# Up pass of a sparse expert layer: low parts made ahead of row fetches, row coefficients spread a group ahead

## Chip, cores and metric

The kernel runs on one core of one Trainium2 chip. The metric is the device time of one execution in microseconds. The median of three runs of the kernel before is 4072.21 us (4071.66 to 4079.16).

## What is computed

The reference is one block of a hybrid network for 1024 tokens of width 1024: an RG-LRU and an SSD mixer, then a feed-forward layer that picks experts. Only that last layer matters here:

```
def peer_ffn(h, w_q, sub_keys, expert_down, expert_up):
    ...
    idx = i1 * PEER_KEYS + i2          # 8 heads x 16 picks of 16384 experts, for each token
    g = jax.nn.softmax(cv, axis=-1)
    u = expert_down[idx]
    act = jax.nn.gelu(jnp.einsum('thkd,td->thk', u, xb).astype(jnp.float32), approximate=False)
    v = expert_up[idx]
    return jnp.einsum('thk,thkd->td', (g * act).astype(xb.dtype), v)
```

The expert tables have 16384 rows of 1024 float32. The last sum, over v, is the up pass, `experts_up`, the last stage of the kernel.

## The kernel before

The up pass treats the eight blocks of 128 tokens in three ways.

**Five dense blocks (640 tokens).** For them the sum over picks is a matrix product with the whole table. The table comes in 128 blocks of 128 experts. A block n = 4g + j belongs to group g of `GROUPS` = 32, with `GT` = 4 blocks each. SP loads the block (`up_raw`, two buffers) and its coefficients (`gelu_in` and `weights_in`, two buffers each; L2305, L2308, L2309). A load of `up_raw` waits until the low part of the block two before is made, a load of coefficients until the low part of the coefficients two before is made. For full precision each operand is split into a high and a low part:

- ScalarE makes `up_hi` (L2400) and `coef_hi` (L2402). Its copies for group g wait until TensorE is through with group g - 2.
- GpSimd makes `up_lo`, in `cut(g, j)` (L2352).
- VectorE multiplies the coefficients (L2466) and makes `coef_lo` (L2468), in `coefs(g, j)`.

TensorE works a group as ten slots (five blocks of tokens by two halves of the width). A slot is twelve matmuls (L2576; in group 0, L2557, the slots go in two halves of five, with the blocks of experts outside). A group begins when all four cuts and all four low parts of the coefficients are made. VectorE adds the slots of group g - 1 to `y_acc` in `add` (L2478; L2475 for group 0) while it prepares group g: slots 0 and 1 after block 0, slots 2 to 4 after block 1, slots 5 and 6 after block 2, slots 7 to 9 after block 3.

**Two blocks of tokens by rows on TensorE.** For each pick of each of 256 tokens one row of the table is gathered, the 128 rows of one token per fetch: `fetch(r)` (L2335) is an indirect DMA of 128 rows of 1024 float32 into one of `RING` = 6 tiles. TensorE takes four such tiles in `quad(n)` (L2538), rows 4n to 4n + 3, with 16 matmuls. Quad 2g stands after slot 0 of group g, quad 2g + 1 after slot 5. The coefficients of a quad are spread by VectorE in `spread_rows(n)` (L2445), into one of four buffers. A row fetch waits until the quad that read its tile before is done. After the 32nd quad ScalarE copies the sums away (`keep_rows`, L2390).

**One block of tokens on VectorE.** `fetch_own(c)` (L2345) gathers row c of 128 tokens into one of two tiles. `add_own(c)` (L2458; L2454 for the first) adds it on VectorE. An own fetch c waits until own add c - 2 is done. VectorE does own add 4(g - 1) + j right after `coefs(g, j)`.

All engines work their queues in order. The order on GpSimd is written out by hand (L2355 to L2382), and the change touches it. In group g of the loop GpSimd issues row fetches 8g - 2 to 8g + 1 (the first four) and 8g + 2 to 8g + 5 (the second four), and own fetches 4g - 2 to 4g + 1.

Of the kernel before, what the change touches and what calls it, by code (L numbers as in the profile page):

```python
# [2238 lines left out]
GT = 4  # L2239
# [3 lines left out]
def experts_up(m, inp, keep, scratch, out):  # L2243
# [6 lines left out]
    GROUPS = E1 // GT  # L2250
    SLOTS = 2 * ND
    BANKS = SLOTS // 2
    NP = NA - 1
# [5 lines left out]
    with ExitStack() as st:  # L2259
# [38 lines left out]
        with nc.Block() as block:  # L2298
            @block.sync
            def _(sp):  # L2300
                for n in range(E1):
                    u = n % 2
                    if n >= 2:
                        sp.wait_ge(up_lo_done, n - 1)
                    sp.dma_start(up_raw[:, u], up[n]).then_inc(up_loaded[u], 16)  # L2305
                    if n >= 2:
                        sp.wait_ge(g_lo_done, n - 1)
                    sp.dma_start(gu[:, u], scratch["gu"][n]).then_inc(gu_loaded[u], 16)  # L2308
                    sp.dma_start(w[:, u], scratch["w"][n]).then_inc(w_loaded[u], 16)  # L2309
                sp.wait_ge(up_lo_done, E1)  # L2310
                for i, t in enumerate(FINISH):
                    if i >= 2:
                        sp.wait_ge(summed, i - 1)
                    sp.dma_start(x1[:, i % 2], scratch["x1"][t * P:(t + 1) * P, :]).then_inc(x1_loaded[i % 2], 16)
                    if i >= 1:
                        b = FINISH[i - 1]
                        sp.wait_ge(summed, i)
                        sp.dma_start(out[0, b * P:(b + 1) * P, :], acc[:, b, :]).then_inc(out_stored, 16)
                b = FINISH[-1]
                sp.wait_ge(summed, TB)  # L2320
                sp.dma_start(out[0, b * P:(b + 1) * P, :], acc[:, b, :]).then_inc(out_stored, 16)
                sp.wait_ge(out_stored, 16 * TB)

            @block.gpsimd
            def _(pool):
                pool.memset(eps[:], EPS).then_inc(eps_set, 1)

                def fetch(r):
                    a, i = divmod(r // 4, QUADS)
                    t = r % 4 * QUADS + i  # L2330
                    if r == 0:
                        pool.wait_ge(ids_ready, 1)
                    if r >= RING:
                        pool.wait_ge(quad_done, (r - RING) // 4 + 1)
                    pool.indirect_dma_start(out=rows[:, r % RING, :], out_offset=None, in_=inp["peer_up"][0],  # L2335
                                            in_offset=bass.IndirectOffsetOnAxis(ap=ids_t[:, a, t:t + 1], axis=0)
                                            ).then_inc(rows_loaded[r % RING], 16)

                def fetch_own(c):

                    if c == 0:
                        pool.wait_ge(own_ids, 1)
                    if c >= RING_OWN:
                        pool.wait_ge(own_added, c - RING_OWN + 1)
                    pool.indirect_dma_start(out=own_rows[:, c % RING_OWN, :], out_offset=None, in_=inp["peer_up"][0],  # L2345
                                            in_offset=bass.IndirectOffsetOnAxis(ap=ids_t[:, OWN, c:c + 1], axis=0)
                                            ).then_inc(own_loaded[c % RING_OWN], 16)

                def cut(g, j):
                    n, u = g * GT + j, j % 2  # L2350
                    pool.wait_ge(up_hi_done, n + 1)
                    pool.tensor_tensor(up_lo[:, g % 2, j, :], up_raw[:, u], up_hi[:, g % 2, j, :].bitcast(F32),  # L2352
                                       ALU.subtract).then_inc(up_lo_done, 1)

                cut(0, 0)  # L2355
                cut(0, 1)
                for r in range(4):
                    fetch(r)
                fetch_own(0)
                cut(0, 2)  # L2360
                cut(0, 3)
                for r in range(4, RING):
                    fetch(r)
                fetch_own(1)
                for g in range(1, GROUPS):
                    r, c = (g - 1) * 4 * NP + RING, (g - 1) * GT + RING_OWN
                    cut(g, 0)
                    fetch_own(c)
                    for i in range(4):
                        fetch(r + i)  # L2370
                    cut(g, 1)
                    fetch_own(c + 1)
                    cut(g, 2)
                    fetch_own(c + 2)
                    for i in range(4, 8):
                        fetch(r + i)
                    cut(g, 3)
                    fetch_own(c + 3)
                for r in range((GROUPS - 1) * 4 * NP + RING, 4 * QUADS * NP):
                    fetch(r)  # L2380
                for c in range((GROUPS - 1) * GT + RING_OWN, P):
                    fetch_own(c)  # L2382
# [43 lines left out]
            def _(dve):  # L2426
# [12 lines left out]
                def spread_rows(n):  # L2439

                    a, i = divmod(n, QUADS)
                    col = coef_t[:, a].rearrange("p (j i) -> p j i", i=QUADS)[:, :, i:i + 1]
                    if n >= SPREADS:
                        dve.wait_ge(quad_done, n - SPREADS + 1)
                    dve.tensor_tensor(spread[:, n % SPREADS], col.to_broadcast([P, 4, QUADS]),  # L2445
                                      one_at[:, QUADS - 1 - i:2 * QUADS - 1 - i].unsqueeze(1).to_broadcast([P, 4, QUADS]),
                                      ALU.mult
                                      ).then_inc(spread_ready, 1)

                def add_own(c):  # L2450

                    dve.wait_ge(own_loaded[c % RING_OWN], 16 * (c // RING_OWN + 1))
                    if c == 0:
                        dve.tensor_scalar(acc[:, OWN, :], own_rows[:, 0, :], coef[:, OWN, 0:1], None, ALU.mult  # L2454
                                          ).then_inc(own_added, 1)
                        return
                    dve.wait_ge(own_added, c)
                    dve.scalar_tensor_tensor(acc[:, OWN, :], own_rows[:, c % RING_OWN, :], coef[:, OWN, c:c + 1],  # L2458
                                             acc[:, OWN, :], ALU.mult, ALU.add).then_inc(own_added, 1)

                def coefs(g, j):
                    n, v, u = g * GT + j, g % 2, j % 2
                    loads = 16 * (n // 2 + 1)
                    dve.wait_ge(gu_loaded[u], loads)
                    dve.wait_ge(w_loaded[u], loads)
                    dve.tensor_tensor(gu[:, u], gu[:, u], w[:, u], ALU.mult).then_inc(coef_ready, 1)  # L2466
                    dve.wait_ge(g_hi_done, n + 1)
                    dve.tensor_tensor(g_lo[:, v, j, :], gu[:, u], g_hi[:, v, j, :].bitcast(F32), ALU.subtract  # L2468
                                      ).then_inc(g_lo_done, 1)

                def add(g, s):
                    dve.wait_ge(y_mm, g * SLOTS + (s + 1))
                    part = acc[:, NA + s // 2, (s % 2) * TH:(s % 2 + 1) * TH]
                    if g == 0:
                        dve.tensor_copy(part, ps_y[s % BANKS][:]).then_inc(added, 1)  # L2475
                    else:
                        dve.wait_ge(added, g * SLOTS + (s + 1 - SLOTS))
                        dve.tensor_tensor(part, ps_y[s % BANKS][:], part, ALU.add).then_inc(added, 1)  # L2478

                for g in range(GROUPS):  # L2480
                    for j in range(GT):
                        coefs(g, j)
                        if g:
                            add_own((g - 1) * GT + j)
                        if g == 0:
                            continue
                        for s in range(j * SLOTS // GT, (j + 1) * SLOTS // GT):
                            add(g - 1, s)
                    for q in range(NP):
                        spread_rows(g * NP + q)  # L2490

                def finish(i):
                    t = FINISH[i]
# [180 lines left out]
```

## Time and profile before

| | busy us | share of the span |
|---|---|---|
| TensorE, matmuls | 3796.6 | 93% |
| TensorE, weight loads | 3193.4 | 79% |
| VectorE | 2708.6 | 67% |
| ScalarE | 1664.8 | 41% |
| GpSimd | 1820.8 | 45% |

The profiled execution took 4068.46 us; its span, first to last instruction, is 4066.7 us. The up pass begins near 2997. In the page's forty slices of the span, the last ten are the up pass; TensorE's digit is nine in most of them, and so is that of the DMA engines, which move some 350 GB/s there. The page gives 18.6 us as TensorE's idle time ahead of the matmuls of L2576, of 4066.7; GpSimd's row fetches (L2335) are idle 91.2 us ahead of them, most of it its own pace of issue.

How to read it: a chain of waits follows the end of the run back through what released each step. A timeline shows one engine's instructions in order, and, in brackets, the idle time before an instruction and what ended it. An indirect DMA's instruction is over after about 1 us; its data lands later, which is told as its time to landing, counted from the instruction's start.

### The profile page before, as it was taken

Reading aid. Unit: us, or ns where it says so; the run is one execution under the profiler, and the core shown is the slowest. Engines: PE = TensorE matmul, PEld = TensorE weight load, DVE = VectorE, ACT = ScalarE, POOL = GpSimd, SP = SyncE. Lnnn points to the kernel's source line nnn. Section 1 sums busy time; section 2 is a strip of 40 time slices with the busy share of each in tenths; the row PEclk is TensorE's granted clock in tenths of the full one; section 3 lists DMA queues with packets and bytes.
Section 4 is the critical chain, followed back from the end, with each engine's and each line's share of the span. In section 5 each row is a group of like instructions: output and inputs, shape, how many; then the busy total and the mean of one; then the engine's idle time right before and its main releaser. Section 6 shows DMA issues by size and latency. Waiting matters only on the chain. (4 is left out here: it accounts for less than half of the span.)

```text
span 4066.7 us, 57361 instructions
## 1 busy us (share of the span) xinstructions
PE 3796.6 (93%) x21102; PEld 3193.4 (79%) x21102; DVE 2708.6 (67%) x4934; ACT 1664.8 (41%) x3225; POOL 1820.8 (45%) x1291
## 2 busy tenths in 40 slices
PE   6999899989899969998999999999969999999998
PEld 3877688866677869998999999999956777777776
DVE  3587411148775426688999999997756666666666
ACT  2111233358422431136777777777612222222222
POOL 3333233359544112133333333335546767676774
PEclk8999899999999989999999999999989999999999
DMA  4244333348666332276888888889999999999998
GB/s 158 69 150 150 120 97 124 103 160 263 183 196 190 103 123 73 62 259 231 269 274 274 266 281 268 271 272 352 364 309 349 352 347 350 336 336 349 347 349 290
DMA packets 641664, 957.80 MB, mean 236 GB/s; under 512 B 198900, under 2 KB 418820, under 8 KB 640516
## 3 DMA queue, kind: packets, MB, share of 16 engines
q1 hardware_dynamic: 311984, 407.35, 30.5%
q0 software_dynamic: 110592, 402.70, 28.3%
q10 hardware_dynamic: 218836, 144.47, 11.3%
q8 instruction: 148, 2.42, 0.2%
q14 instruction: 104, 0.85, 0.1%
HBM read 807.46 MB, written 146.93 MB: 235 GB/s over the span
## 5 line engine op out<-in xcount | busy, mean ns | idle before, releaser
L2034 POOL DMA_INDIRECT down_rows<-in_peer_down_dram,row_ids x384 | 464.3, 1209 | 830.3 <-DVE row_u L2174 743.4
L2055 PE MATMUL p_u<-h2T_hi,downT_hi 128*128 128x320 f32 x2048 | 657.2, 321 | 11.3 <-ACT gelu_out L2105 10.6
L2055 PE MATMUL p_u<-h2T_lo,downT_hi 128*128 128x320 f32 x2048 | 637.6, 311 | 0.0
L2055 PE MATMUL p_u<-h2T_hi,downT_lo 128*128 128x320 f32 x2048 | 637.3, 311 | 0.0
L2174 DVE CUSTOM_DVE_ANT_0 gate_rows<-down_rows,x_tok_rows 128x1024 f32<-128x1024 f32 x384 | 469.1, 1222 | 79.8 <-DMA down_rows<-in_peer_down_dram,row_ids 66.7
L2576 PE MATMUL p_y<-up_hi,coef_hi 128*128 128x512 f32 x1240 | 493.3, 398 | 18.6 <-DVE coef_lo L2468 9.2
L2576 PE MATMUL p_y<-up_lo,coef_hi 128*128 128x512 f32 x1240 | 485.9, 392 | 0.0
L2576 PE MATMUL p_y<-up_hi,coef_lo 128*128 128x512 f32 x1240 | 483.9, 390 | 0.0
L545 PE MATMUL p<-hT_hi,w_hi 128*128 128x512 f32 x1024 | 410.4, 401 | 7.1 <-POOL w_lo L499 7.1
L2055 PEld LDWEIGHTS p_u<-h2T_hi,downT_hi 128*128 128x128 f32 x2048 | 390.2, 191 | 13.7 <-issue 12.7
L545 PE MATMUL p<-hT_hi,w_lo 128*128 128x512 f32 x1024 | 399.9, 391 | 0.0
L545 PE MATMUL p<-hT_lo,w_hi 128*128 128x512 f32 x1024 | 399.8, 390 | 0.0
L2055 PEld LDWEIGHTS p_u<-h2T_lo,downT_hi 128*128 128x128 f32 x2048 | 390.0, 190 | 0.0
L2055 PEld LDWEIGHTS p_u<-h2T_hi,downT_lo 128*128 128x128 f32 x2048 | 388.9, 190 | 0.0
L2478 DVE TENSOR_TENSOR y_acc<-p_y,y_acc 128x512 f32<-128x512 f32 x310 | 212.3, 688 | 204.8 <-PE p_y L2576 204.7
L2352 POOL TENSOR_TENSOR up_lo<-up_raw,up_hi 128x1024 fp32r<-128x1024 f32 x128 | 322.2, 2518 | 30.3 <-ACT up_hi L2400 28.5
L2576 PEld LDWEIGHTS p_y<-up_hi,coef_hi 128*128 128x128 f32 x1240 | 233.5, 188 | 122.4 <-issue 61.7
L2335 POOL DMA_INDIRECT up_rows<-in_peer_up_dram,row_ids_turned x256 | 268.1, 1047 | 91.2 <-issue 76.9
L2402 ACT CAST coef_hi<-gelu_in 128x640 fp32r<-128x640 f32 x128 | 93.1, 728 | 485.1 <-DVE gelu_in L2466 485.1
L497 POOL CAST w_hi<-w_raw 128x1024 fp32r<-128x1024 f32 x64 | 68.1, 1065 | 497.2 <-issue 319.5
L2576 PEld LDWEIGHTS p_y<-up_hi,coef_lo 128*128 128x128 f32 x1240 | 233.7, 188 | 50.5
L2576 PEld LDWEIGHTS p_y<-up_lo,coef_hi 128*128 128x128 f32 x1240 | 233.8, 189 | 46.3
(337 smaller groups left out, 8081.1 us busy)
## 6 DMA issues: line engine op xcount, KB each, us to landing
down_raw<-in_peer_down_dram SPq DMA_DIRECT2D x128, 512.0 KB, 5.6
up_raw<-in_peer_up_dram SPq DMA_DIRECT2D x128, 512.0 KB, 5.7
scratch_gu<-gelu_out ACTq DMA_DIRECT2D x128, 320.0 KB, 5.1
gelu_in<-scratch_gu SPq DMA_DIRECT2D x128, 320.0 KB, 6.1
weights_in<-scratch_w SPq DMA_DIRECT2D x128, 320.0 KB, 6.9
w_raw<-in_w_in_dram SPq DMA_DIRECT2D x64, 512.0 KB, 4.2
scratch_w<-weights_out ACTq DMA_DIRECT2D x40, 512.0 KB, 8.1
scratch_w<-y_acc ACTq DMA_DIRECT2D x40, 512.0 KB, 7.0
```

The costliest lines, as they stand in the source:

```text
L497: pool.tensor_copy(w_hi[:, u], w_raw[:, u]).then_inc(hi_done, 1)
L545: mm = pe.matmul(ps[u][:, half, :], w[:, u, k, :], hT[h][:, k, half * TH:(half + 1) * TH], start=(n == 0), stop=(n == 3 * KD - 1))
L2034: pool.indirect_dma_start(out=rows[:, c % RING, :], out_offset=None, in_=inp["peer_down"][0], in_offset=bass.IndirectOffsetOnAxis(ap=row_i ...
L2055: mm = pe.matmul(ps_u[half][:, 0:HD], d[:, n % 3, k, :], h2[h][:, k, half * HD:(half + 1) * HD], start=(j == 0), stop=(j == 3 * KD - 1))
L2174: dve.tensor_tensor_reduce(junk, rows[:, c % RING, :], x_tok[:, a], 1.0, 0.0, ALU.mult, ALU.add, row_u[:, a, k:k + 1]).then_inc(dot_done, 1)
L2335: pool.indirect_dma_start(out=rows[:, r % RING, :], out_offset=None, in_=inp["peer_up"][0], in_offset=bass.IndirectOffsetOnAxis(ap=ids_t[: ...
L2352: pool.tensor_tensor(up_lo[:, g % 2, j, :], up_raw[:, u], up_hi[:, g % 2, j, :].bitcast(F32), ALU.subtract).then_inc(up_lo_done, 1)
L2402: act.copy(g_hi[:, v, j, :], gu[:, u]).then_inc(g_hi_done, 1)
L2478: dve.tensor_tensor(part, ps_y[s % BANKS][:], part, ALU.add).then_inc(added, 1)
L2576: mm = pe.matmul(ps_y[s % BANKS][:], a[:, v, j, t * P:(t + 1) * P], b[:, v, j, half * TH:(half + 1) * TH], start=(n == 0), stop=(n == 3 * ...
```

## The change

On GpSimd, in the groups from 1 on, the order within a group changes. Before it was cut 0, own fetch, four row fetches, cut 1, own fetch, cut 2, own fetch, four row fetches, cut 3, own fetch. After, it is cut 0, own fetch, four row fetches, cut 1, own fetch, cut 2, own fetch, cut 3, own fetch, four row fetches. In group 1 the first four row fetches come after cut 2 and its own fetch, too.

On VectorE, the coefficients of quads 0 and 1 are spread before group 0. Those of group g + 1 are spread at the end of group g, where before those of group g were. The last group spreads nothing.

```
                 for g in range(1, GROUPS):
                     r, c = (g - 1) * 4 * NP + RING, (g - 1) * GT + RING_OWN
-                    cut(g, 0)
-                    fetch_own(c)
-                    for i in range(4):
-                        fetch(r + i)
-                    cut(g, 1)
-                    fetch_own(c + 1)
-                    cut(g, 2)
-                    fetch_own(c + 2)
-                    for i in range(4, 8):
-                        fetch(r + i)
-                    cut(g, 3)
-                    fetch_own(c + 3)
+                    for j in range(GT):
+                        cut(g, j)
+                        fetch_own(c + j)
+                        if j == (2 if g == 1 else 0):
+                            for i in range(4):
+                                fetch(r + i)
+                        if j == 3:
+                            for i in range(4, 8):
+                                fetch(r + i)
...
+                for q in range(NP):
+                    spread_rows(q)
                 for g in range(GROUPS):
                     for j in range(GT):
                         coefs(g, j)
...
-                    for q in range(NP):
-                        spread_rows(g * NP + q)
+                    if g + 1 < GROUPS:
+                        for q in range(NP):
+                            spread_rows((g + 1) * NP + q)
```

## Rows read from the trace of the kernel before

**Rows 1.** Chain of waits: start us, us, what (a steady group; gaps)
```profile
3271.87 1.85 PE p_rows L2538 x16
3273.72 13.87 PE p_y L2576 x60
3287.59 1.85 PE p_rows L2538 x16
...
3379.33 0.72 issue
...
3537.50 4.56 issue
3542.06 5.23 PE p_y L2576 x12
```

**Rows 2.** Timeline of TensorE, groups 0 and 1: start, us, instruction [idle before]
```profile
3031.36 0.71 PE L2557 MATMUL p_y<-up_hi,coef_hi 128*128 128x512 f32 x1 [2.77 <-DVE y_acc L2475]
...
3036.44 0.50 PE L2557 MATMUL p_y<-up_hi,coef_hi 128*128 128x512 f32 x1 [2.24 <-DVE y_acc L2475]
...
3047.69 1.92 PE L2538 MATMUL p_rows<-up_rows,row_spread 128*32 128x512 f32 x16
...
3062.44 0.80 PE L2576 MATMUL p_y<-up_hi,coef_hi 128*128 128x512 f32 x1 [9.20 <-DVE coef_lo L2468]
...
3067.44 1.92 PE L2538 MATMUL p_rows<-up_rows,row_spread 128*32 128x512 f32 x16 [0.51 <-DVE row_spread L2445]
```

**Rows 3.** Timeline of GpSimd, its group 8 and the start of group 9
```profile
3269.86 2.40 POOL L2352 TENSOR_TENSOR up_lo<-up_raw,up_hi 128x1024 fp32r<-128x1024 f32 x1
3276.03 0.95 POOL L2345 DMA_INDIRECT up_own_rows<-in_peer_up_dram,row_ids_turned  x1 [3.78 <-DVE y_acc L2458]
...
3278.53 0.93 POOL L2335 DMA_INDIRECT up_rows<-in_peer_up_dram,row_ids_turned  x1 [0.30 <-issue]
...
3281.96 2.42 POOL L2352 TENSOR_TENSOR up_lo<-up_raw,up_hi 128x1024 fp32r<-128x1024 f32 x1
...
3291.13 0.96 POOL L2345 DMA_INDIRECT up_own_rows<-in_peer_up_dram,row_ids_turned  x1 [2.15 <-DVE y_acc L2458]
```

**Rows 4.** Timeline of VectorE, blocks 2 and 3 of its group 8
```profile
3269.79 3.16 DVE L2466 TENSOR_TENSOR gelu_in<-gelu_in,weights_in 128x640 f32<-128x640 f32 x1
...
3274.48 1.28 DVE L2458 SCALAR_TENSOR_TENSOR y_acc<-up_own_rows,row_coef,y_acc 128x1024 f32<-128x1024 f32 x1
...
3276.74 0.69 DVE L2478 TENSOR_TENSOR y_acc<-p_y,y_acc 128x512 f32<-128x512 f32 x1 [0.38 <-PE p_y L2576]
3277.35 0.82 DVE L2466 TENSOR_TENSOR gelu_in<-gelu_in,weights_in 128x640 f32<-128x640 f32 x1
...
3279.71 1.32 DVE L2458 SCALAR_TENSOR_TENSOR y_acc<-up_own_rows,row_coef,y_acc 128x1024 f32<-128x1024 f32 x1
```

**Rows 5.** Timeline of ScalarE, its copy for the last cut of group 8
```profile
3273.89 1.05 ACT L2400 CAST up_hi<-up_raw 128x1024 fp32r<-128x1024 f32 x1 [0.18 <-DMA up_raw<-in_peer_up_dram]
```

**Rows 6.** Row fetches by their tile: all 256, then the one of 3278.53
```profile
DMA to landing us min/median/max: 4.4/6.1/11.4
...
DMA to landing us min/median/max: 5.6/5.6/5.6
```

**Rows 7.** Timeline of VectorE, own add in block 3 of its group 16
```profile
3536.21 1.28 DVE L2458 SCALAR_TENSOR_TENSOR y_acc<-up_own_rows,row_coef,y_acc 128x1024 f32<-128x1024 f32 x1
```

**Rows 8.** Timeline of GpSimd, group 1: own fetch 2 and cut(1, 1)
```profile
3030.97 0.95 POOL L2345 DMA_INDIRECT up_own_rows<-in_peer_up_dram,row_ids_turned  x1 [3.25 <-DVE y_acc L2454]
...
3045.68 2.40 POOL L2352 TENSOR_TENSOR up_lo<-up_raw,up_hi 128x1024 fp32r<-128x1024 f32 x1
```

**Rows 9.** Timeline of ScalarE, its copy for cut(1, 1)
```profile
3029.09 1.04 ACT L2400 CAST up_hi<-up_raw 128x1024 fp32r<-128x1024 f32 x1
```

**Rows 10.** Timeline of VectorE, group 1: product of block 1, own add of block 2
```profile
3032.15 0.83 DVE L2466 TENSOR_TENSOR gelu_in<-gelu_in,weights_in 128x640 f32<-128x640 f32 x1 [0.25 <-DMA weights_in<-scratch_w]
...
3039.85 1.28 DVE L2458 SCALAR_TENSOR_TENSOR y_acc<-up_own_rows,row_coef,y_acc 128x1024 f32<-128x1024 f32 x1
```

## Prediction

> **What bounds the kernel now.** I read the page first: TensorE is busy 93% of the span, and from the thirtieth slice on, where the up pass runs, the DMA row shows nines. So I looked for TensorE's idle time in the up pass. Four names are used below. A *cut* is GpSimd's making of one low part (L2352). A *row fetch* is L2335, and a *quad* is TensorE's use of four fetched row tiles (L2538). An *own fetch* (L2345) feeds VectorE's *own add* (L2458). In cut(g, j), g is the group and j the block in it.
>
> The chain of waits shows a steady pass: each group of 31.44 us is twice a quad of 1.85 and sixty matmuls of 13.87 [rows 1]. In the whole pass there are few exceptions. One gap of 9.20 us stands at the start of group 1 [rows 2], one of 4.56 at group 16, and four of 0.7 like the one at 3379.33 [rows 1].
>
> Then I read, engine by engine, what runs up to the start of group 9, at 3284.9. GpSimd's last cut of the group runs 3281.96 to 3284.38 [rows 3]. It ends 0.5 us before TensorE needs it, so this is the tight place today; the change takes hold of it. VectorE's last block is not tight: it starts when add 6 of the group before, 3276.74, is out, and its own add ends at 3281.03 [rows 4].
>
> **What is moved, and what it queues behind.** In each group from the second on, the last cut and the own fetch after it go ahead of the second four row fetches. The cut alone has what it needs: ScalarE's copy for it is done at 3274.94 [rows 5]. It would run from 3276.98, the end of the own fetch of 3276.03, to 3279.4, and be 5 us early. SP's next load of up_raw, which waits for that cut, goes out 5 us earlier too, from 3284.4 to 3279.4. No bytes are added.
>
> The own fetch is another matter. Own fetch c waits until own add c-2 has emptied the buffer. For the last one of a group that is the own add of VectorE's block 3, which ends at 3281.03 [rows 4]. In the kernel before, this fetch stood behind the four row fetches and waited for nothing. Now the four row fetches stand behind it on the same in-order engine. The first two of them bring rows 8g+2 and 8g+3, and quad 2g, at slot 1 of the next TensorE group, waits for both. This is the new wait. Behind quad 2g on TensorE everything queues.
>
> Worked out at group 8: the own add ends at 3281.03. An own fetch starts 0.27 after its own add (3275.76 to 3276.03), and the second row fetch starts 2.50 after the own fetch (3276.03 to 3278.53) [rows 3, 4]. So row 8g+3 is issued at 3283.8 instead of 3278.53. A row fetch lands 4.4 to 11.4 us after issue, median 6.1; this very one took 5.6 [rows 6]. I take 5.85, midway, because the loads ahead of it keep the distances they have now: up_raw goes out when a cut ends, 3272.26 today, 3.8 us before the own fetch of 3276.03 [rows 3], and gu and w when VectorE's low part is out, just before the own add of 3274.48 [rows 4]. The row lands at 3289.65. The quad now starts at 3287.59 [rows 1]. TensorE stands **2.1 us**; with 5.6 and 6.1 it is 1.8 and 2.3.
>
> Does the loop give this back? No. After the quad, slots 1 to 5, the other quad and slot 6 follow at TensorE's own pace, and slot 6 starts VectorE's add, product, own add, and so the fetch again. Slot 6 to quad is 13.0 us by this path against 10.9 by TensorE's own. So each group costs 2.1 anew: groups 2 to 31 without 16 are 29, **+61 us**.
>
> *Group 16.* There ScalarE stops to copy the row sums, and cut(16, 3) ends late; TensorE stands 4.56 and then takes 5.23 for twelve matmuls [rows 1]. The moved cut removes that. But the own add there ends at 3537.49 [rows 7]; with 2.77 and 5.85 the rows land at 3546.1, and the quad is at 3547.29 today. The early cut will meet VectorE's product (below), for about 1.5. So **0**: one wait takes the other's place.
>
> *The four gaps of 0.7*, 1.0 each with the restart, and some shorter ones are late cuts, and vanish into the new wait: **-5 us**.
>
> *Start.* In group 1 cut(1, 1) waits today behind four row fetches until 3045.68 [rows 8]; ScalarE's copy for it is done at 3030.13 [rows 9]. In the change it runs from 3031.92, the end of the own fetch. There VectorE's product of 3032.15 [rows 10] meets it. What that costs I read at 3269.79: a product that starts beside a cut of 3269.86 takes 3.16 us, not 0.82, and ends about 0.7 behind the cut [rows 3, 4]. So the product ends near 3035.0, 2.1 late. The next product meets cut(1, 2) likewise, and the own add behind it, which ends at 3041.1 today [rows 10], loses 2.1 and some 1.8 more and ends at 3045.0. Own fetch 4 and then rows 6 and 7 follow: row 7 is issued at 3047.8 and lands at 3053.6. Quad 1 stands at 3047.69 today [rows 2]: 6 us late. From there: slot 6's add some 3.3 us later, 4.3 to the end of the own add, 2.8 to the fetch, 5.85 to land: 3069.9. Quad 2 stands at 3067.44 today. The 9.20 gap goes, and a larger one comes: **+3 us**, between 0 (landings of 4.4) and +8.
>
> *Spreads.* The first two move from the end of group 0 to its head, where VectorE waits for the first loads anyway. Later ones are the same instructions at the same place, one group ahead. The buffers are four and the quads whose slots they reuse are long done. The only thing TensorE ever waited for there is 0.51 us at 3067.44 [rows 2]; it hides behind the row wait: **0**, between -0.5 and +0.5.
>
> Sum: 61 + 0 - 5 + 3 = +59 us. Against the profiled execution, 4068.5 (span 4066.7), that is 4127.5. The median of the runs is 3.7 higher, 4072.2, so the forecast is **4131**.
>
> **The clock.** A stand of 2.1 us should leave TensorE at its upper level: after a gap of 2.24 the first matmul record is 0.50, close to the warm ones, while after 2.77 it is 0.71 [rows 2], and after 4.56 twelve matmuls take 5.23 instead of 2.8 [rows 1]. So a stall much over 2.1 also pays the slow clock, 1.2 to 2.5 us. This is why the range is longer upward.
>
> **Rivals.**
> *The lock of cut and product.* The moved cut would end at 3279.4, and VectorE's product starts at 3277.35. If they meet, the product is 2.1 late and the stall 4.2, with the slow clock behind it: 29 x (2.1 + 1.2) = +96, 4227. Against it: once TensorE stands, GpSimd's first half of the group, which hangs on the group's start and not on the quad, moves ahead of the quad by the stall. That goes up to 2.6, since the group's first row fetches wait for quad 2g, which ends at 3289.44 [rows 1], and the own fetch before them ends at 3292.09 [rows 3]. Cut(g, 2) then ends before its product, and cut(g, 3) runs from about 3274.9 to 3277.3, just ahead of 3277.35. That is a margin of 0.1 us, so part of it may come: 4160 to 4227. The Trainium skill (SBUF — State Buffer, "Who interferes with whom") says that such a two-input VectorE operation and a GpSimd one that reads SBUF lock each other out for a whole instruction, by order of issue; the trace's 3.16 against 0.82 agrees.
>
> *Faster landings.* With 2 us more per group for the same bytes the queues could drain. With the shortest landing seen, 4.4 [rows 6], the stall is 0.6: 29 x 0.6 - 5 + 0 = +12, 4085.
>
> *The faster side.* The point where it turns is a landing of 3.8 us (3287.59 - 3283.8). Below it the quad is never late and only the gains stay: -7 at group 16 (4.56 and 2.5 of slow clock), -5, and -3 to -8 at the start, since the last block of group 1 no longer waits for its late load: 4052 to 4057. Against it: none of 256 row fetches landed in under 4.4. The Trainium skill (DMA: Bandwidth & Descriptors, "Anatomy of one DMA — SWDGE (gpsimd) path") fits a transfer issued by GpSimd by 2.0 us plus its bytes over 436 GB/s. For 512 KB that gives 3.2 us, and by it the change would be faster; the trace, with the queues full, shows 6.1.
>
> *It does nothing.* Landings near 4 us would cancel gains against stalls: within 0.2% of 4072.
>
> **How the numbers follow.** Forecast 4131, with 4112 to 4160 for its own bounds (1.5 to 2.8 us a group, start 0 to +8): 0.65. Lock and slow clock, above 4160: 0.14. Faster landings, 4081 to 4112: 0.10. Nothing: 0.03. Faster: 0.08. The range that holds 8 in 10 is 4095 to 4175. A difference of 0.2%, 8 us, is about what measurement can tell. Faster 0.08, same 0.03, slower 0.89.
>
> **What the changed profile would show.** In the chain of waits every 33.5 us, not 31.44, with the second part of a group's quad released by a row DMA. On GpSimd the last own fetch of each group after an idle stretch that ends with VectorE's own add, and the four row fetches right behind it. The last cut done 7 us before the group starts. No gap of 9.20 at group 1's start but late quads 1 and 2. A granted clock near 1.00 in the steady part. The prediction is wrong if the stall per group is absent though GpSimd's order is as described (landings under 3.8), or if the products grow to 3 us in block 3 (the lock).

## The result and the profile after

The changed kernel takes 4199.3 us in the median of four runs (4177.5 to 4236.0); the kernel before takes 4072.1 (4071.7 to 4079.2). The ratio is 1.032, 95% interval 1.025 to 1.038: slower by 127 us, where I had forecast slower by 59. The profiled execution is the slowest of the four (span 4234.3 us), so rows from it give per-group figures that lie somewhat above the median's.

TensorE's longest wait in the up pass, in the changed kernel (engine and line, released by: us in total, times, longest):

```profile
PE p_rows L2538 <- DMA up_rows<-in_peer_up_dram,row_ids_turned: 109.9, 32, 7.4
```

This line does not exist in the kernel before. It is the wait that was forecast, and it comes in every group: 3.4 us in the mean, not 2.1. The steady part before and after, by windows (us; busy time of TensorE, its weight loads, VectorE, ScalarE, GpSimd; TensorE's granted clock; DMA share; GB/s). First before, then after:

```profile
3100.00:3500.00 400.00, 399.28 (x1930) 294.13 (x1923) 272.54 (x304) 88.96 (x102) 280.66 (x204) 1.00 0.96 351
```

```profile
3100.00:3500.00 400.00, 363.11 (x1642) 259.93 (x1641) 249.03 (x261) 73.35 (x86) 236.57 (x175) 0.92 0.88 298
```

TensorE idles 37 of 400 us, its mean granted clock is 0.92, and the transfers fall from 351 to 298 GB/s. Neither TensorE nor the DMA engines are as full as before; the pass runs at the speed of a chain of waits. The chain of waits of the changed kernel, for one group (start us, us, what):

```profile
4029.29 1.29 DVE y_acc L2455
...
4030.84 0.96 POOL up_own_rows L2345
...
4032.10 0.94 POOL up_rows L2335
...
4033.34 6.33 DMA up_rows<-in_peer_up_dram,row_ids_turned
...
4039.81 3.64 PE p_rows L2538 x16
4043.45 14.64 PE p_y L2576 x60
4058.10 1.85 PE p_rows L2538 x16
4059.95 3.00 PE p_y L2576 x12
...
4062.97 0.03 DVE y_acc L2475
...
4063.58 2.26 DVE gelu_in L2463
...
4067.37 1.29 DVE y_acc L2455
...
4068.92 0.96 POOL up_own_rows L2345
...
4071.43 5.71 DMA up_rows<-in_peer_up_dram,row_ids_turned
...
4077.28 3.64 PE p_rows L2538 x16
```

Read it against [rows 1]. Own add (now L2455), own fetch, row fetch, landing, quad, slots 1 to 6, add 6, product (L2463), own add: the loop of the forecast, link by link. From quad 4039.81 to quad 4077.28 it takes 37.47 us instead of 31.44. Where the 6.03 us are:

- 3.46 us between add 6 and the quad: 14.31 (4062.97 to 4077.28), where the kernel before has 10.85 (3276.74 [rows 4] to 3287.59 [rows 1]). Of them 1.44 are the product, 2.26 here against 0.82 [rows 4]. The other 2.0 are the forecast's 2.1.
- 1.79 us in the quad, 3.64 against 1.85 [rows 1], and 0.77 in the sixty matmuls behind it, 14.64 against 13.87: TensorE comes out of its stand at the lower level of its clock (granted 0.50 over these 3.64 us).

Products met cuts before the change, too. From group 2 on (duration in ns, min/median/max), in the kernel before:

```profile
L2466 DVE TENSOR_TENSOR gelu_in<-gelu_in,weights_in x116: 810/821/3426, 3097.3 to 4012.3; 128x640 f32<-128x640 f32 x116
```

The long ones are those of block 2, like the 3.16 us of 3269.79 [rows 4]: 29 of 30 took over 1.2 us. The last cut, which comes behind them, still ended in time, by 0.5 us at 3284.38. What is new is that block 3's product meets the moved cut: its median goes from 0.82 to 2.06 us, 28 of 30 take over 1.2, and the own fetch ahead of the rows waits for the own add behind it. GpSimd and VectorE in the changed kernel, up to the stand of 4039.81 (timelines: start, us, instruction, idle time before it):

```profile
4011.96 2.40 POOL L2352 TENSOR_TENSOR up_lo<-up_raw,up_hi 128x1024 fp32r<-128x1024 f32 x1
4016.52 0.95 POOL L2345 DMA_INDIRECT up_own_rows<-in_peer_up_dram,row_ids_turned  x1 [2.16 <-DVE y_acc L2455]
4017.49 2.41 POOL L2352 TENSOR_TENSOR up_lo<-up_raw,up_hi 128x1024 fp32r<-128x1024 f32 x1
4023.68 0.96 POOL L2345 DMA_INDIRECT up_own_rows<-in_peer_up_dram,row_ids_turned  x1 [3.77 <-DVE y_acc L2455]
4024.65 2.41 POOL L2352 TENSOR_TENSOR up_lo<-up_raw,up_hi 128x1024 fp32r<-128x1024 f32 x1
4030.84 0.96 POOL L2345 DMA_INDIRECT up_own_rows<-in_peer_up_dram,row_ids_turned  x1 [3.78 <-DVE y_acc L2455]
```

```profile
4011.72 3.34 DVE L2465 TENSOR_TENSOR coef_lo<-gelu_in,coef_hi 128x640 fp32r<-128x640 f32 x1 [0.80 <-ACT coef_hi L2399]
...
4018.28 2.32 DVE L2463 TENSOR_TENSOR gelu_in<-gelu_in,weights_in 128x640 f32<-128x640 f32 x1
...
4025.84 1.92 DVE L2463 TENSOR_TENSOR gelu_in<-gelu_in,weights_in 128x640 f32<-128x640 f32 x1
```

All three own fetches wait for an own add; in the kernel before the last of them waited for nothing. Each ends 1.2 us after its own add, and a cut follows at once. VectorE meanwhile does an add or two and comes to its next product 0.8 to 1.2 us after the cut has begun. So an own add that releases an own fetch with a cut behind it also times that cut to start just ahead of the next product, and the product waits for it.

### The profile page after: what moved, and what is told of

Same layout as the page of the kernel before. It is cut to its first block and busy times, and to the rows that moved or that the text cites. A ratio compares the mean times of both kernels' runs of the same rounds, so it can differ in the third digit from the quotient of the medians.

```text
span 4234.3 us, 57361 instructions
## 1 busy us (share of the span) xinstructions
PE 3859.9 (91%) x21102; PEld 3213.4 (76%) x21102; DVE 2767.4 (65%) x4934; ACT 1658.5 (39%) x3225; POOL 1791.1 (42%) x1291
## 5 line engine op out<-in xcount | busy, mean ns | idle before, releaser
L2576 PE MATMUL p_y<-up_hi,coef_hi 128*128 128x512 f32 x1240 | 502.4, 405 | 3.8 <-DVE coef_lo L2465 2.3
L2352 POOL TENSOR_TENSOR up_lo<-up_raw,up_hi 128x1024 fp32r<-128x1024 f32 x128 | 310.9, 2429 | 17.3 <-ACT up_hi L2397 15.0
L2335 POOL DMA_INDIRECT up_rows<-in_peer_up_dram,row_ids_turned x256 | 259.0, 1012 | 126.0 <-issue 72.9
```

Of the source, the lines that this page charges most:

```text
L2576: mm = pe.matmul(ps_y[s % BANKS][:], a[:, v, j, t * P:(t + 1) * P], b[:, v, j, half * TH:(half + 1) * TH], start=(n == 0), stop=(n == 3 * ...
```

## Experiments

In the runs on other chips the kernel before has medians of 4074 to 4077 us, so the ratios count. "Of before" below is the ratio with its 95% interval.

**own_last**: the second four row fetches directly behind the last cut, the own fetch behind them.

```
 for j in range(GT):
     cut(g, j)
+    if j == 3:
+        for i in range(4, 8): fetch(r + i)
     fetch_own(c + j)
     if j == (2 if g == 1 else 0):
         for i in range(4): fetch(r + i)
-    if j == 3:
-        for i in range(4, 8): fetch(r + i)
```

> The changed kernel, with one thing moved: in each group the last own fetch goes behind the second four row fetches again, so that these follow the last cut directly. Theory (the row fetches are late because an own fetch ahead of them waits for VectorE's own add): the second of the four is issued at about 3281 on the clock of the kernel before instead of 3283.8, lands near 3287, and quad 2g finds its rows: 4060 to 4080 us. Rival (it is the moving of the row fetches behind the last cut, or the crowding of transfers after it, that makes the rows late): nearly all of the loss stays, 4150 us or more.

Measured: 4096.3 us, 1.0059 of before (1.0042 to 1.0076). Four fifths of the loss are gone, so the wait of the own fetch carries it; but 22 us stay, more than the expectation of 4060 to 4080 allowed. Block 3's products still meet a cut (median 1.95 us, 28 of 30 over 1.2), yet the row fetches for the next quad no longer stand behind the own add that follows. Its chain of waits shows why:

```profile
3122.77 2.41 POOL up_lo L2352
...
3125.34 1.36 POOL up_rows L2335
...
3127.00 7.75 DMA up_rows<-in_peer_up_dram,row_ids_turned
...
3134.89 1.92 PE p_rows L2538 x16
```

The end of the cut releases SP's load of up_raw at the same moment as the row fetches behind it, and the rows land after 7.75 us (median of 22 such links of the chain 7.8, against 5.8 for 28 in the changed kernel). The next loads of coefficients go out half a microsecond after the row fetch of 3127.00, too. No run holds these loads back, so that they slow the rows, the crowding rival, fits the times but is not shown. In the changed kernel the landings were as forecast.

**own_ring3**: the order of the changed kernel with three tiles for own rows. The row numbers stay in `row_f`, so that name stands in its rows of the trace.

```
-    RING_OWN = 2
+    RING_OWN = 3
...
-        coef = m.sb(st, "row_coef", [P, NA, P])
+        coef = row_u
...
-        ids_t = m.sb(st, "row_ids_turned", [P, NA, P], U32)
+        ids_t = row_f[:].bitcast(U32)
...
                 fetch_own(1)
+                fetch_own(2)
```

> The order of the changed kernel, untouched, but three tiles for own rows instead of two (room is made by keeping the row coefficients and row numbers in the tiles that they are computed from). An own fetch then waits for the own add three before it, not two before. Theory: the wait behind which the row fetches stand is gone, the second of them is issued about 1 us later than in own_last, lands near 3288, and TensorE stands 0 to 1 us per group at the upper clock: 4065 to 4100 us. Rival (order of the fetches by itself): 4150 us or more.

Measured: 4195.8 us, 1.0319 of before (1.0286 to 1.0351): no gain at all. The edit was wrong, not the theory. The start of the rows in a group, c = (g - 1) * 4 + `RING_OWN`, moved with the ring, so every place of the order fetched the next row and waited for the very same own add.

**ring3_same** mends that: c = (g - 1) * 4 + 2 again, without the third early fetch.

> As own_ring3, three tiles for own rows in the order of the changed kernel, but each own fetch fetches the row that it fetches there, so that it now really waits for an own add one earlier: the last one of a group waits for the own add of block 2, done when the last cut is over. (In own_ring3 each place of the order fetched the next row into the added tile and so waited for the very same own add.) Theory: TensorE's stand falls by the wait for block 3's own add, some 3 us; what stays is like own_last plus one own fetch ahead of the rows, 1.3 to 2.5 us: 4105 to 4160 us. Rival (the wait of the own fetch is not what counts): 4185 us or more.

Measured: 4079.9 us, 1.0015 of before (1.0006 to 1.0025). GpSimd's order is that of the changed kernel, instruction for instruction; the edit changes the waits of its own fetches alone, and the loss is 6 us instead of 130. The last cut and the own fetch after it, in group 2, first in own_ring3, then in ring3_same:

```profile
3094.72 2.40 POOL L2352 TENSOR_TENSOR up_lo<-up_raw,up_hi 128x1024 fp32r<-128x1024 f32 x1
3100.91 0.96 POOL L2345 DMA_INDIRECT up_own_rows<-in_peer_up_dram,row_f  x1 [3.78 <-DVE y_acc L2456]
3102.17 0.94 POOL L2335 DMA_INDIRECT up_rows<-in_peer_up_dram,row_f  x1 [0.30 <-issue]
```

```profile
3091.35 3.29 POOL L2352 TENSOR_TENSOR up_lo<-up_raw,up_hi 128x1024 fp32r<-128x1024 f32 x1 [0.96 <-ACT up_hi L2397]
3094.78 0.96 POOL L2345 DMA_INDIRECT up_own_rows<-in_peer_up_dram,row_f  x1
3096.05 0.94 POOL L2335 DMA_INDIRECT up_rows<-in_peer_up_dram,row_f  x1 [0.30 <-issue]
```

The 3.78 us are gone, and with them the meeting in block 3, whose product takes 0.82 us in most groups. So this run takes away both parts of the loss together. TensorE waits for rows 11 times in that pass, not 32:

```profile
PE p_rows L2538 <- DMA up_rows<-in_peer_up_dram,row_f: 16.8, 11, 6.2
```

My expectation, 4105 to 4160, was too slow. I had taken one own fetch off its wait, but all of them come off, so the cuts ahead of the last one start earlier too.

**half_cut**: the changed kernel with cuts of half the columns.

```
-  pool.tensor_tensor(up_lo[:, g % 2, j, :], up_raw[:, u], up_hi[:, g % 2, j, :].bitcast(F32),
+  pool.tensor_tensor(up_lo[:, g % 2, j, 0:TH], up_raw[:, u, 0:TH], up_hi[:, g % 2, j, 0:TH].bitcast(F32),
```

> The changed kernel, with each low part of the table made for the first half of its columns alone and used for both halves (so half of the low parts is wrong): a cut takes about 1.2 us instead of 2.4, everything else stays. Theory (the part of the loss that the forecast lacks comes from the products that start beside a cut and wait for it, and from the slow clock that follows a longer stall): products of block 3 fall back to about 0.8 us, the stall per group to about 2.1, the clock mostly stays up: 4105 to 4145 us. Rival (the extra loss has another cause, such as later landings): 4180 us or more.

Measured: 4138.9 us, 1.0167 of before (1.0145 to 1.0188), inside the expectation. Products from group 2 on (duration in ns, min/median/max), in the changed kernel and in half_cut:

```profile
L2463 DVE TENSOR_TENSOR gelu_in<-gelu_in,weights_in x118: 811/2026/3710, 3093.2 to 4176.0; 128x640 f32<-128x640 f32 x118
```

```profile
L2463 DVE TENSOR_TENSOR gelu_in<-gelu_in,weights_in x117: 815/817/2618, 3090.5 to 4078.6; 128x640 f32<-128x640 f32 x117
```

The median falls from 2026 to 817 ns, with 4 of 117 over 1.2 us, and TensorE's wait for rows from 109.9 to 71.0 us:

```profile
PE p_rows L2538 <- DMA up_rows<-in_peer_up_dram,row_ids_turned: 71.0, 32, 6.4
```

That is 2.2 us each: the stand of the forecast, in a kernel whose products hardly ever meet a cut. Most groups whose quad takes 1.92 us last 32.9 to 34.1 us, where the forecast had 33.5.

**half_before**: the same half cuts in the kernel before, the control.

> The kernel before with the half low parts of half_cut (the second half of the columns uses the low parts of the first): what the shorter cuts are worth by themselves. Theory: TensorE is bound elsewhere, so only the late cuts at the ends of groups, the wait at group 16 and part of the start go: 4055 to 4068 us, and the stand per group in half_cut is then (4139 minus this) over 30, 2.3 to 2.8 us. Rival (shorter cuts speed up much more, and half_cut says nothing on products that meet cuts): under 4050 us.

Measured: 4059.6 us, 0.9959 of before (0.9943 to 0.9974), inside the expectation. The shorter cuts give 17 us by themselves. half_cut ran on another chip; it is 65 us above the kernel before there, so with half cuts the change costs 65 + 17 = 82 us, with whole cuts 127. In the forecast's terms the half-cut pair should show 61 for the groups and 3 for the start, without the -5 for late cuts, which half_before no longer has (29 groups of 31.44 us): 64, against 82. In the two profiled executions the 82 are 75 in the 29 groups, 3 at group 16 and 4 at the start. The 14 us above 61 are mostly the clock: eight of half_cut's 30 quads behind a stand took 2.75 to 3.6 us, and these groups last 34.8 to 35.4. The other 45 us of the 127 come with the length of the cuts: products that wait for them, and the slow clock that a longer stand brings. These two are not separated by a run.

**spread_only**: VectorE's part of the change alone, in the kernel before.

```
+  for q in range(NP):
+      spread_rows(q)
   for g in range(GROUPS):
...
-      for q in range(NP):
-          spread_rows(g * NP + q)
+      if g + 1 < GROUPS:
+          for q in range(NP):
+              spread_rows((g + 1) * NP + q)
```

> The kernel before with the change on VectorE alone: quads 0 and 1 spread ahead of group 0, those of the next group at the end of each. Theory: nothing hangs on it, 4072 us within 2; the 0.51 us that TensorE waited for a spread at quad 2 is gone. Rival (the spreads ahead delay VectorE where it counts): some 10 us or more slower.

Measured: 4076.4 us, 1.0007 of before (0.9997 to 1.0016): no difference that ten runs can tell. The 0.51 us at quad 2 are gone, as expected. By this run the loss is GpSimd's part.

**group1_only** and **rest_only**: GpSimd's new order in group 1 alone, and in groups 2 to 31 alone.

```
+  if g == 1:      # rest_only: if g > 1
       (the new order)
+  else:
+      (the order of before)
```

> The changed kernel with its new GpSimd order in group 1 alone; groups 2 to 31 have the order of before. Theory (start term of the forecast, +3 us, with the late cuts of the other groups left as they are): 4070 to 4082 us. Rival (the new order of group 1 gains what the wait of 9.2 us cost): 4058 to 4068 us.

> The changed kernel with group 1 in the order of before and the new order from group 2 on. Theory: the loss is made anew in every group, and the start had only +3 us of it: 4185 to 4205 us. Rival (the late start of group 1 sets the phase in which cuts and products meet, and a better start keeps them apart): 4130 to 4160 us.

Measured: group1_only 4080.3 us, 1.0015 of before (1.0006 to 1.0025), 6 us slower with an interval of 2 to 10, inside the expectation; rest_only 4206.1, 1.0335 (1.0309 to 1.0361), 1 us above its range and far from the rival's. The whole loss is made anew in each group from 2 on, whatever the start was. In the profile of group1_only quad 1 is late just as in the forecast's start: the row fetch goes behind an own fetch that waits for an own add behind a product that meets a cut.

```profile
3041.50 2.53 DVE gelu_in L2477
...
3045.55 1.29 DVE y_acc L2469
...
3047.11 0.96 POOL up_own_rows L2345
...
3049.61 6.16 DMA up_rows<-in_peer_up_dram,row_ids_turned
...
3055.91 1.92 PE p_rows L2552 x16
```

**split_fetch** and **split_start**: what the change is after, without the new wait. The two row fetches that quad 2g needs, the last cut, the other two, the own fetch. In split_start, group 1's first four row fetches come after its second cut.

```
   for j in range(GT):
+      if j == 3:
+          for i in range(4, 6): fetch(r + i)
       cut(g, j)
+      if j == 3:
+          for i in range(6, 8): fetch(r + i)
       fetch_own(c + j)
-      if j == (2 if g == 1 else 0):
+      if j == 0:      # split_start: (1 if g == 1 else 0)
           for i in range(4): fetch(r + i)
-      if j == 3:
-          for i in range(4, 8): fetch(r + i)
```

> The changed kernel with the second four row fetches of each group split around the last cut: the two that quad 2g needs, the last cut, the other two, then the own fetch; group 1 in the same order. Theory: rows 8g+2 and 8g+3 go as early as in the kernel before and the last cut ends 2.5 us earlier, so the late cuts vanish and no new wait comes: 4058 to 4070 us. Rival (any earlier cut meets a product, delays VectorE and crowds the transfers, and costs more than it gives): 4078 us or more.

> split_fetch, and in group 1 the first four row fetches after the second cut instead of the first. Theory: the second cut of group 1 fills GpSimd's wait of 9 us for quad 0, the loads behind it go out 13 us earlier and TensorE's 9.2 us at the start of group 1 shrink to 2 to 5, less some 2 us for the product that meets the cut: 3 to 7 us below split_fetch. Rival: the product that meets the cut delays quads 0 and 1 so that no gain is left: within 2 us of split_fetch.

Measured: 4070.8 and 4070.6 us, 0.9989 (0.9979 to 0.9999) and 0.9987 (0.9978 to 0.9997) of before: 4 to 5 us faster each, at the edge of what is measured, split_fetch 1 us above its range. split_start gains nothing over split_fetch in the median, as its rival said, but the rival's reason is not borne out by the profiled executions: quad 2 comes 69.6 us after the pass's first matmul, against 71.5 in split_fetch, so the start gains 1.9 us, and group 16 loses 1.6 again. In split_fetch TensorE has its clock at 1.00 and nothing idle from 3100 to 3500:

```profile
3100.00:3500.00 400.00, 400.00 (x1939) 294.97 (x1941) 304.56 (x307) 87.35 (x102) 286.39 (x205) 1.00 0.97 351
```

That does not hold to the end. Counted from quad to quad, its groups after about 3740 take 31.5 to 33.2 us, and over the pass they lose 4.2 us on 31.44, where the kernel before loses 4.7 in its late cuts. What split_fetch gains is at group 16: 34.0 us from quad 30 to quad 32, against 38.5 before.

**ring3_split**: both remedies, the split order from group 2 on and three tiles for own rows (ring3_same); in group 1 the order of the changed kernel.

> Three tiles for own rows and the own fetches of ring3_same, the order of the changed kernel in group 1, and from group 2 on the order of split_fetch (two row fetches, last cut, two row fetches, own fetch). Theory: group 1 starts as early as in ring3_same (quad 2 came 64.7 us after the pass began there, 70.7 in the kernel before), and the later groups run at 31.44 us as in split_fetch: 4055 to 4065 us where before is 4075. Rival (the gains at the start and in the steady part stand for the same slack, and only one is had): 4068 to 4074 us.

Measured: 4057.1 us (4048.8 to 4062.2), 0.9947 of before (0.9934 to 0.9961), inside the expectation. It beats both kernels: 20 us faster than before on its chip, and some 140 than the change. Of the 15 us that its profiled execution gains within the pass on that of the kernel before, 5 are at the start, 5 at group 16 and 5 the late cuts; every other group takes 31.44. Its GpSimd and its VectorE in group 9:

```profile
3308.17 2.40 POOL L2352 TENSOR_TENSOR up_lo<-up_raw,up_hi 128x1024 fp32r<-128x1024 f32 x1
```

```profile
3308.88 2.39 DVE L2469 TENSOR_TENSOR gelu_in<-gelu_in,weights_in 128x640 f32<-128x640 f32 x1
```

Here the product meets the last cut and takes 2.38 or 2.39 us in each of groups 3 to 10, and these groups still take 31.44. A product that meets a cut cost nothing here, where nothing that TensorE needs soon hangs on the own add behind it.

## Why the prediction was wrong in size

**The mechanism was right.** The step on which it rests, the own fetch that goes ahead of the row fetches and waits for block 3's own add, is shown three ways: by the chain of waits, by own_last, and by ring3_same, which takes away this kind of wait and nothing of the order. (What the forecast calls the start of group 9, at 3284.9, is TensorE's group 8; nothing in the sum hangs on the name.)

**The term of 2.1 us per group** is right as a price of that wait alone: the landing was taken as 5.85 us and is 5.8 in the median of the chain; the stand without the product's part is 2.0 in the group shown, and 2.2 in half_cut. As the whole cost of a group it is the term that was mis-sized. The forecast had 61 - 5 = 56 us for the 29 groups; between the two profiled executions they are 154, 5.3 us a group.

**The step that failed** is the one that dismissed the lock of cut and product. It said that once TensorE stands, GpSimd's first half moves ahead of the quad, cut(g, 2) ends before its product, and cut(g, 3) just ahead of 3277.35. It went wrong in two places. First, the move is limited by quad 2g's end, and with the slow clock that comes 1.8 us later than I had reckoned (3.64 against 1.85). Second, I moved GpSimd and VectorE as if each had its own time. But each of the last two cuts follows an own fetch that VectorE's own add has just released, so a cut and the next product start within about 1.2 us of each other: 4017.49 and 4018.28, then 4024.65 and 4025.84. The rival that I gave 0.14 was the case, with the product 1.1 to 1.4 us late, not 2.1. Its price for one collision was too high, and its price for the clock too low.

The first of the two places is not enough by itself. Two quads of the changed kernel kept the upper level, at 3226.43 and 3485.31, and block 3's next products still took 1.56 and 1.54 us, before stands of 3.35 and 3.32. Cut and product did part behind longer stands. The two longest but group 16's, 4.31 and 4.00, were followed by products of 1.02 and 0.87 and by stands of 2.12 and 1.76, as the forecast had expected for every group. (Group 16's 7.16 was followed by a product of 2.04.) The second case in the chain of waits:

```profile
3449.76 3.64 PE p_rows L2538 x16
...
3473.32 0.88 DVE gelu_in L2463
...
3485.31 1.92 PE p_rows L2538 x16
```

So in these groups the stand moved the cut out of the way only at some 4 us, not at 2.1, and behind the shorter stand that followed the meeting came back.

**The clock.** I wrote that 2.1 us would not lower it and a stall much over that would cost 1.2 to 2.5. It cost 1.79 + 0.77 = 2.6 in the group shown, after a stand of 3.74:

```profile
4039.81 3.64 PE L2538 MATMUL p_rows<-up_rows,row_spread 128*32 128x512 f32 x16 [3.74 <-DMA up_rows<-in_peer_up_dram,row_ids_turned]
```

So the two surplus terms are 1.4 and 2.6 us in this group. Over 29 groups that would be 116 us; the profiled execution, 4236, lies 105 above the forecast. The median run has 37 us less, and it left no trace. The mean granted clocks of the four runs go with their times: 0.955 at 4236 us, 0.962 at 4206, 0.964 at 4193, 0.969 at 4178. In the profiled one the groups around 3226 and 3500 take 34.8 to 35.8 us, most others 36 to 38.

**Start: +3 us** forecast. In the profiled executions quad 2 is 3.8 us later than before, counted from the pass's first matmul, in the changed kernel and 3.2 in group1_only. The forecast left out the slow clock behind that stand; with it group1_only gives 6 (2 to 10). **Spreads: 0**; spread_only gives 2 (-1 to 7), not told from none. **The late cuts, -5:** in the kernel before the groups other than 16 lose 4.7 us on 31.44 each, in ring3_split and half_before nothing, so the size was right. **Group 16, 0:** one wait did take the other's place, but a larger one. From quad 30 to quad 32 the changed kernel takes 41.8 us, the one before 38.5, so +3; the stand there is 7.16 us:

```profile
3633.13 3.64 PE p_rows L2538 x16
```

With these terms the two profiled executions add up: 154 for the groups, 3 for group 16, 4 for the start, 1 behind the last groups, and 6 ahead of the pass make the 168 us between their spans. The 6 are not the change's: the kernels are the same up to there, and in the other runs that are, the pass begins anywhere between 2997.6 and 3005.6.

**The rival of short landings** fell: with 298 GB/s instead of 351 the rows land in 5.8 us, not in 4.4. A lower total rate did not shorten the landing here; the long landings, 7.8 in own_last, are those with a load of up_raw issued beside the fetch.

## What to carry to other kernels

When an instruction is moved ahead of others on an in-order engine, list the waits of everything that moves with it: here the cut was ready, and the own fetch that travelled along was not. When two engines whose operations wait for each other's end also release each other, as here, the operations can meet in every round; a forecast must walk one full round of the loop on both engines, with the longer durations in it, before it calls a meeting avoided. And if a wait is to be removed by another buffer, keep what each place fetches: a prefetch that grows with the ring waits for the same event as before.

## What the runs showed of the hardware

With a stand of TensorE of some 3.4 us in every group of about 37 us its mean granted clock was 0.92 from 3100 to 3500. Of the 30 stands before quads from group 2 on in the changed kernel (1.8 to 7.2 us), 25 were followed by a quad of 3.2 to 3.64 us, all or most of it at the lower level, three by one of 2.4 to 2.7, and two by one of 1.92, all at the upper level. In half_cut (1.4 to 5.7 us, mean 2.1) 22 of 30 quads took 1.92 and eight 2.75 to 3.6. The length of the stand alone does not decide. In own_ring3 a quad of 3.43 us came after a stand of 2.01, and in rest_only 12 quads of 1.92 after stands of 1.99 to 3.82.

Two indirect fetches land in 5.8 us in the median when the load of up_raw went out 3 to 4 us before the own fetch ahead of them (changed kernel, 298 GB/s). They land in 7.8 us when it goes out at the same moment (own_last, 342 GB/s, still below the 351 of the kernel before). The nine late row fetches in ring3_same's chain of waits from group 2 on, issued just behind such a load as well, take 8.0; these are the ones that TensorE had to wait for, so they are not a fair sample of all.
